# Experts taken in inner blocks of 1024 columns, with half of the small experts' gate units multiplied unsplit in plain fp32

## The reference

```python
def swiglu(xn, w_gate, w_up, w_down):
    return (jax.nn.silu(xn @ w_gate) * (xn @ w_up)) @ w_down

def moe_swiglu(xn, w_router, w_gate, w_up, w_down):
    logits = (xn @ w_router).astype(jnp.float32)
    top_v, top_i = lax.top_k(logits, TOP_K)
    top_w = jax.nn.softmax(top_v, axis=-1)
    gates = jnp.sum(jax.nn.one_hot(top_i, N_EXPERTS, dtype=jnp.float32) * top_w[..., None], axis=-2)
    out = jnp.zeros_like(xn)
    for e in range(N_EXPERTS):
        ye = swiglu(xn, w_gate[e], w_up[e], w_down[e])
        out = out + gates[..., e:e + 1].astype(xn.dtype) * ye
    return out
```

## Time and profile before

| | |
|---|---|
| time, median of 3 runs (range) | 1371.85 us (1371.69 to 1371.88) |
| the profiled execution's own time | 1372.46 us |
| its span, first to last instruction | 1370.7 us |
| busy: PE, PEld, DVE, ACT, POOL | 97%, 79%, 84%, 69%, 5% |
| mean granted TensorE clock | 0.997 of full speed |
| moved by DMA | 422.46 MB |
| chain that ended last: PE, DVE, ACT, issue | 75%, 16%, 4%, 3% |
| splits `split_lo` (DVE) of 2048 columns | 382, together 868.0 us |
| splits `split_hi` (ACT) of 2048 columns | 385, together 732.4 us |

### The profile page before, as it was taken

The page is one execution under the profiler, slowest core; times in us unless marked ns, Lnnn a source line. Parts: engine busy times, 40 slices in busy tenths (PEclk is TensorE's granted clock), DMA queues, the critical chain, the costliest instruction groups (busy, mean ns, idle before and its releaser), DMA issues.

```text
span 1370.7 us, 17261 instructions
## 1 busy us (share of the span) xinstructions
PE 1325.2 (97%) x6404; PEld 1083.2 (79%) x6404; DVE 1154.4 (84%) x970; ACT 951.4 (69%) x874; POOL 71.5 (5%) x110
## 2 busy tenths in 40 slices
PE   8999999999998999999999999999999999999998
PEld 7776888888886887777777767788888888888887
DVE  6897655557888989999999999998898899889886
ACT  5676544446775777777777777777777777776775
POOL 2120910000200000000000000000000000000000
PEclk9999999999999999999999999999999999999999
DMA  8743765555298989999999999999999999999980
GB/s 301 268 131 84 259 205 191 184 186 170 76 368 308 336 299 367 388 395 394 393 393 390 377 394 395 391 362 382 334 354 369 372 359 363 383 332 338 381 325 31
DMA packets 197860, 422.46 MB, mean 308 GB/s; under 512 B 13064, under 2 KB 37392, under 8 KB 197776
## 3 DMA queue, kind: packets, MB, share of 16 engines
q1 hardware_dynamic: 197776, 421.35, 85.1%
HBM read 420.27 MB, written 1.05 MB: 307 GB/s over the span
## 4 chain that ended last, share of the span: by engine, by line
PE 75%; DVE 16%; ACT 4%; issue 3%; SPq 1%; DMA 1%; POOL 0%; ACTq 0%; DVEq 0%; POOLq 0%
PE ps L334 20%; PE ps L336 19%; PE ps L335 19%; DVE w_lo L314 11%; PE ps L885 5%; ACT w_hi L297 3%; PE ps L883 3%; PE ps L1048 1%; PE ps L865 1%; PE ps L1023 1%; PE ps L1049 1%; PE ps L862 1%; PE ps L882 1%; DMA raw<-in_attn_w_qkv_dram 1%; DVE resid L2128 1%
## 5 line engine op out<-in xcount | busy, mean ns | idle before, releaser
L314 DVE TENSOR_TENSOR w_lo<-raw,w_hi 128x2048 fp32r<-128x2048 f32 x382 | 868.0, 2291 | 132.0 <-ACT w_hi L297 130.7
L297 ACT ACTIVATE w_hi<-raw 128x2048 fp32r<-128x2048 f32 x385 | 732.4, 1914 | 127.9 <-PE ps L336 105.5
L334 PE MATMUL ps<-w_hi,xe 128*128 128x512 f32 x448 | 179.2, 400 | 6.9 <-DVE w_lo L314 6.9
L336 PE MATMUL ps<-w_hi,xe 128*128 128x512 f32 x448 | 175.2, 391 | 0.0
L335 PE MATMUL ps<-w_lo,xe 128*128 128x512 f32 x448 | 175.2, 391 | 0.0
L334 PE MATMUL ps<-w_hi,h_t_hi 128*128 128x512 f32 x360 | 141.0, 392 | 0.3 <-DVE w_lo L314 0.3
L336 PE MATMUL ps<-w_hi,h_t_lo 128*128 128x512 f32 x360 | 140.3, 390 | 0.0
L335 PE MATMUL ps<-w_lo,h_t_hi 128*128 128x512 f32 x360 | 140.1, 389 | 0.0
L334 PE MATMUL ps<-w_hi,xb 128*128 128x512 f32 x280 | 111.5, 398 | 1.9 <-DVE w_lo L314 1.9
L885 PE MATMUL ps<-a_all,w_hi 128*128 128x512 f32 x308 | 109.8, 396 | 0.0
L336 PE MATMUL ps<-w_hi,xb 128*128 128x512 f32 x280 | 109.2, 390 | 0.0
(11 more groups left out here) (319 smaller groups left out, 1854.2 us busy)
## 6 DMA issues: line engine op xcount, KB each, us to landing
raw<-in_moe_w_gate_dram SPq DMA_DIRECT2D x112, 1024.0 KB, 7.8
raw<-in_moe_w_up_dram SPq DMA_DIRECT2D x111, 1024.0 KB, 7.9
raw<-in_moe_w_down_dram SPq DMA_DIRECT2D x111, 1024.0 KB, 7.5
raw<-in_attn_w_qkv_dram SPq DMA_DIRECT2D x11, 1024.0 KB, 12.3
raw<-in_ffn_w_gate_dram SPq DMA_DIRECT2D x11, 1024.0 KB, 5.3
raw<-in_ffn_w_up_dram SPq DMA_DIRECT2D x11, 1024.0 KB, 5.4
raw<-in_ffn_w_down_dram SPq DMA_DIRECT2D x11, 1024.0 KB, 4.9
raw<-in_ple_w_gate_dram SPq DMA_DIRECT2D x8, 1024.0 KB, 7.0
```

The source lines that it names most:

```text
L297: nc.scalar.activation(w_hi[:, u % SPLIT, :], raw_slot(u), ACT.Copy).then_inc(hi_ready, 1)
L314: nc.vector.tensor_tensor(w_lo[:, u % SPLIT, :], raw_slot(u), w_hi[:, u % SPLIT, :].bitcast(F32), ALU.subtract).then_inc(lo_ready, 1)
L334: nc.tensor.matmul(out, x[0], w[0], start=first, stop=False)
L336: return nc.tensor.matmul(out, x[1], w[0], start=False, stop=last)
```

## The change

**Blocks.** The hidden columns are taken in four blocks of 1024, 1024, 1024 and 512 columns. A gate or up unit of a wide block is 2 chunks of 1024 columns (4 KB runs in memory) in place of 4 of 512. A wide block has 4 gate, 4 up and up to 4 down units of the block before; the blocks of a turn have 10, 12, 12 and 8 units. silu, product and transposes' sources are 1024 wide, the two halves' hidden parts lie in `h_t` and `p_t`; silu stands behind the split of unit 6 of the block, the product behind that of unit 10.

**Whole units.** In turns 1 to 3 the last two gate units of each wide block and the last gate unit of the narrow one (`WHOLE`, 7 of 42 units, 21 in all) are not split. TensorE waits for their landing alone and multiplies the raw weights in plain fp32 by `x_whole`, an unsplit copy of the tokens that ScalarE makes when it gathers them; their slot of `raw` comes free when TensorE has used them.

**Scatter.** All four quarters of a result go through bank 5: quarter q waits until quarter q-1 has been added. TensorE issues them in the second block behind units 2, 3, 5 and 6, VectorE adds them behind the splits of units 5, 6, 8 and 9 (`SCATTER_AT`, `ADD_AT`).

**Turn 0.** The sort goes to the second block behind the split of unit 4, the placing of gates and slots behind that of unit 7, and the two row splits behind those of units 11 and 13. The gathers are four pieces in three banks, one ahead of each down unit of the last block; ScalarE, not VectorE, copies the transposed picks.

```diff
+BLOCKS = 4
+BLOCK_AT = (0, 10, 22, 34)
+HALVES = (2, 2, 2, 1)
...
+WHOLE_WIDE, WHOLE_NARROW = (2, 3), (1,)
+WHOLE = [U_TURN + PER_EXPERT * (t - 1) + BLOCK_AT[b] + i for t in FEW_AT for b in range(BLOCKS)
+         for i in (WHOLE_WIDE if HALVES[b] == 2 else WHOLE_NARROW)]
...
         def split_hi(u, k=0, by=None):
 
+            if whole(u, k):
+                return
             load_wait(nc.scalar, u, k)
...
                 before_it = ring(u) - RAW
-                split_wait(eng, before_it if before_it < U_WIDE else before_it + EXTRA, k)
+                before_it = before_it if before_it < U_WIDE else before_it + EXTRA
+                if whole(before_it, k):
+                    eng.wait_ge(unit_used, before_it + 1 + PER_EXPERT * k)
+                else:
+                    split_wait(eng, before_it, k)
             eng.dma_start(dst, view).then_inc(landed[ring(u) % RAW], 16)
...
-                                  for half in range(2)]
+                for b in range(BLOCKS):
+                    views = []
+                    for w in (ge, ue):
+                        n0, n = 1024 * b, 512 * HALVES[b]
+                        chunk = 4 // HALVES[b]
+                        views += [expert_rows(w, e, c0, chunk, n0, n) for c0 in range(0, KD, chunk)]
+                    if b or not first:
+                        before_it = (b - 1) % BLOCKS
+                        views += [expert_rows(de, e if b else e_before, 8 * before_it + 2 * j, 2, 0, D)
+                                  for j in range(2 * HALVES[before_it])]
                     units += [(u + n, view) for n, view in enumerate(views)]
...
 
                 pe.wait_ge(y_lo_ready, t + 1 + k)
                 pe.wait_ge(pick_t_copied, t + 1 + k)
-                if q < 2 and t % 2 == 0:
-                    pe.wait_ge(xe_lo_ready, 2 * (t + 3 + k))
-                elif q < 2:
-                    pe.wait_ge(added, 4 * (t + k))
-                else:
-                    pe.wait_ge(added, 4 * (t + k) + q - 1)
+                if q:
+                    pe.wait_ge(added, 4 * (t + k) + q)
                 tt, half = q // 2, q % 2
                 for y, stop in ((y_hi, False), (y_lo, True)):
-                    last = nc.tensor.matmul(ps[:, 5 + q % 2, :], pick_t[:, tt * P:(tt + 1) * P],
+                    last = nc.tensor.matmul(ps[:, 5, :], pick_t[:, tt * P:(tt + 1) * P],
                                             y[:, 512 * half:512 * half + 512], start=not stop, stop=stop)
...
+            def gate_or_up(t0, b, n, i, k=0, few=False):
+
+                x, width = xb if t0 == 2 else xe, 512 * HALVES[b]
+                chunks = 4 // HALVES[b]
+                u = block_unit(t0, b) + n * KD // chunks + i
+                unit(u, k)
+                if b == 0 and n == 0 and t0 < 2:
+                    pe.wait_ge(xe_lo_ready, 2 * (t0 + k) + (i + 1 if t0 else i // 2 + 1))
+                if i == 0:
+                    pe.wait_ge((silu_ready, hidden_ready)[n], JF + BLOCKS * t0 + b + BLOCKS * k)
+                for c in range(chunks):
+                    d = chunks * i + c
+                    for half in range(HALVES[b]):
+                        out, w = ps[:, 6 * n + half, :], weights(u, c, 512 * half, 512, width)
+                        first, stop = d == 0, d == KD - 1
+                        if few and whole(u, k):
+                            at = c * width + 512 * half
+                            last = nc.tensor.matmul(out, x_whole[:, t0 - 1, d, :], raw_slot(u)[:, at:at + 512], start=first, stop=stop)
+                        elif few and n == 1:
+                            last = product_few(out, x[:, 2 * d * P + FEW:2 * d * P + FEW + P], w, first, stop)
+                        else:
+                            last = product(out, (x[:, 2 * d * P:(2 * d + 1) * P], x[:, (2 * d + 1) * P:(2 * d + 2) * P]), w,
+                                           first, stop)
+                last.then_inc(unit_used, 1)
+
+            def transpose_picks(t0, k=0):
...
-                        transpose_hidden(g, k, few)
+                for b in range(BLOCKS):
+                    units = 2 * HALVES[b]
+                    before_it, t_before = (b - 1) % BLOCKS, t0 if b else t0 - 1
+                    few_then = few if b else few_before
+                    late = t0 == 0 and b == 1
+                    for n in range(2):
+                        for i in range(units):
+                            gate_or_up(t0, b, n, i, k, few)
+                            if (n, i) == ((0, 2) if late else (0, 0)) and (t0 or b):
+                                transpose_hidden(t_before, before_it, 0, k, few_then)
+                            if (n, i) == ((1, 1) if late else (1, 0)) and (t0 or b) and HALVES[before_it] == 2:
+                                transpose_hidden(t_before, before_it, 1, k, few_then)
+                            if b == 1 and t0 and (n, i) in SCATTER_AT:
+                                scatter(SCATTER_AT.index((n, i)), t0 - 1, k)
+                            if b == 2 and (n, i) == (0, 1):
+                                transpose_picks(t0, k)
+                    if b == 1 and t0:
+                        pe.wait_ge(y_lo_ready, t0 + k)
+                    if b or t0:
+                        u = block_unit(t0, b) + 2 * units
+                        for j in range(2 * HALVES[before_it]):
+                            if b == BLOCKS - 1 and t0 != 1:
+                                gather_piece(j, t0, k)
+                            down(u + j, before_it, j, half_at(t_before, before_it), k, few=few_then)
+                            if end and b == BLOCKS - 1 and j == 1:
+                                transpose_hidden(t0, b, 0, k)
+
+            SCATTER_AT = ((0, 2), (0, 3), (1, 1), (1, 2))
 
             pe.wait_ge(xs_ready, XS_AT[4] + 4)
             gather_first()
...
+            def silus(t0, b, k=0):
+                at = JF + BLOCKS * t0 + b
+                used(block_unit(t0, b) + 2 * HALVES[b] - 1, k)
+                act.wait_ge(hidden_ready, at + BLOCKS * k)
+                if HALVES[b] == 2:
+                    nc.scalar.activation(two(expert_silu), ps[:, 0:2, :], ACT.Silu).then_inc(silu_ready, 1)
+                else:
+                    nc.scalar.activation(expert_silu[:, 0:512], ps[:, 0, :], ACT.Silu).then_inc(silu_ready, 1)
+
...
+                for b in range(BLOCKS):
+                    u, units = block_unit(t0, b), 2 * HALVES[b]
+                    before_it, t_before = (b - 1) % BLOCKS, t0 if b else t0 - 1
+                    few_then = few if b else few_before
+                    late = t0 == 0 and b == 1
+                    wide, wide_before = HALVES[b] == 2, HALVES[before_it] == 2
+                    for n in range(0 if b or t0 else 1, 2 * units + (2 * HALVES[before_it] if b or t0 else 0)):
                         split_lo(u + n + AHEAD, k)
-                        if t0 == 0 and f == 1 and n == 1:
-                            hidden_lo(g - 1, k)
-                    hiddens(g, u + 3, k)
-                    if f == 1 and t0:
-                        add_result(0, t0 - 1, k)
-                        add_result(1, t0 - 1, k)
-                    if f == 2:
-                        if t0 == 0:
-                            for tt in range(TT):
-                                dve.wait_ge(rows_split_hi, tt + 1)
-                                cols = slice(tt * D, (tt + 1) * D)
-                                nc.vector.tensor_tensor(a_lo[:, cols], xs[:, tt, :], a_hi[:, cols].bitcast(F32),
-                                                        ALU.subtract).then_inc(rows_split_lo, 1)
+                        if n == 1 and b == 1 and t0:
+                            result_lo(t0 - 1, k)
+                        if n == (3 if late else 1) and (t0 or b):
+                            hidden_lo(t_before, before_it, 0, k, few_then)
+                        if n == ((7 if late else 6) if wide else 4) and (t0 or b) and wide_before:
+                            hidden_lo(t_before, before_it, 1, k, few_then)
+                        if n == ((8 if t0 or b else 7) if wide else 4):
+                            hiddens(t0, b, k)
+                        if b == 1 and t0 and n in ADD_AT:
+                            add_result(ADD_AT.index(n), t0 - 1, k)
+                        if late and n == 2:
                             sort_experts()
-                        dve.wait_ge(pick_transposed, t0 + 1 + k)
-                        nc.vector.tensor_copy(pick_t[:, :], ps[:, 7, 0:TT * P]).then_inc(pick_t_copied, 1)
-                    if f == 3 and t0 != 1:
-                        dve.wait_ge(pick_transposed, t0 + 1 + k)
-                        picks(t0 + 1, 0, k, few=few_next[0])
-                        picks(t0 + 2, 1, k, few=few_next[1])
-                    if f == FB - 1 and t0 != 1:
-                        pair_lo(0, t0, k)
-                    if f or t0:
-                        split_lo(u + 4 + AHEAD, k)
```

(26 more changed lines are left out.)

308 lines of the change are left out of this document (143 added, 165 removed).

## The result

| | us, median | lowest to highest | ratio to before | 95% interval of the ratio |
|---|---|---|---|---|
| before | 1371.88 | 1371.69 to 1373.66 | | |
| after | 1425.54 | 1423.66 to 1428.78 | 1.0391 | 1.0378 to 1.0403 |

The change makes the kernel 53.7 us slower. The prediction said 1413, in a range from 1384 to 1430: the time lies in the range, but over the forecast's own band (1404 to 1420) and in that of its rival 1 (1420 to 1432).

What follows compares the result with a forecast made beforehand. The prediction took full turns as bound by TensorE and small turns as hanging on VectorE's splits. From the median 1371.85, -4.7 (turn 0) + 27.5 (small turns) + 19.2 (scatters) = +42.0 gave 1413 us, range 1384 to 1430.

Steps and rivals of the forecast that it cites:

- the forecast's own band: Whole kernel: the time falls in 1404 to 1420 us, given a chance of 0.50.
- rival 1: Second blocks of turns: the clock falls at the new waits, 7 x 1.4 = +9.8 us, giving 1423; chance 0.12.
- Whole units: Small turns: 3.44 us a unit against 2.78 split, 21 add 13.9 us to TensorE; VectorE can't use all it is spared.
- The wide block: Wide small block of 12 units: 33.1 us against 31.1 for two earlier blocks, 2 us slower.
- Scatters: Second block: quarters 1 and 3 wait for adds, 2.35 and 2.45 us in full turns (+19.2 over four), 1.2 and 3.1 in small.
- Small turns together: Turns 1 to 3: longer by 9.2, 8.6 and 9.0 us, with 0.7 at the seam, +27.5 in sum.
- Turn 0: Turn 0: TensorE's stop and slow clock, 7.0 us, become 2.3 by the new order: -4.7, at worst 0, at best -7.
- The sum takes it as kept: TensorE's clock: assumed to stay at 1.00 through new waits of 2.4 to 3.1 us, so no cost was added.
- PEclk at 1.00 behind the waits: Full turns: TensorE's clock stays at 1.00 behind two waits for adds of 2.3 us each.
- the seam: Where turn 1 follows turn 0, whose down units are full: another 0.7 us.
- Rival 2: Only one loss is real: early enough adds give 1384 to 1395, or small turns add only +14, 1400; chance 0.20.
- Rival 3: Small turns: VectorE catches up during whole units with more than two split units in hand, adds hide, -15, 1357; chance 0.14.

Runs made afterwards that it cites:

- both: The changed kernel with the four adds one split earlier in VectorE's list and no whole units: 1370.20 us, 0.9979 of before.
- the clock held: The changed kernel with unread bf16 matmuls on a free bank ahead of the waits of scatter quarters 1 and 3: 1414.28 us, 1.0304 of before.

## Why the prediction was right, and where its sum was short

Step by step, by the prediction's own terms:

- **Whole units: right.** Two of them in a row take 6.9 us, 3.44 each, as worked out from the earlier trace rows. The first line shows their first six instructions:

```profile
573.67 2.74 PE L1123 MATMUL ps<-raw,xs 128*128 128x512 f32 x6
...
580.13 0.79 PE L1085 MATMUL ps<-w_hi,xe 128*128 128x512 f32 x1
```

  They start at 573.67, and the second matmul behind them starts at 580.77, one step of 0.23 after 580.54 (the record of the first, at 580.13, overlaps the last of them). Leaving out all 21 gave back 13.8 us, and putting 21 into before cost 14.9; the term said 13.9. That VectorE can't use what it is spared shows in its timeline, where each split beside whole units waits for ScalarE, and ScalarE, at 580.80, for the whole unit:

```profile
575.65 2.29 DVE L338 TENSOR_TENSOR w_lo<-raw,w_hi 128x2048 fp32r<-128x2048 f32 x1 [3.98 <-ACT w_hi L319]
579.30 2.29 DVE L338 TENSOR_TENSOR w_lo<-raw,w_hi 128x2048 fp32r<-128x2048 f32 x1 [1.36 <-ACT w_hi L319]
582.75 2.29 DVE L338 TENSOR_TENSOR w_lo<-raw,w_hi 128x2048 fp32r<-128x2048 f32 x1 [1.15 <-ACT w_hi L319]
```

```profile
580.80 1.92 ACT L319 ACTIVATE w_hi<-raw 128x2048 fp32r<-128x2048 f32 x1 [1.25 <-PE ps L1123]
582.62 1.00 ACT L1437 ACTIVATE tmp<-ps 128x1024 f32<-128x1024 f32 x1
583.52 3.79 ACT L319 ACTIVATE w_hi<-raw 128x2048 fp32r<-128x2048 f32 x2
```

- **The wide block: right in time, wrong in its name.** The walk through it gave 33.1; it took 33.35 (566.93 to 600.28), the narrow one 21.65 where 21.6 was said, and the silu does stand between the high parts of units 6 and 7. The prediction set its 2 us over before down to eight units of 8 matmuls in a row, as if width were the cause. Without whole units the same wide block of "both" takes 31.97 (559.50 to 591.47) against 31.1: 1.4 of the 2.2 are the two whole units and 0.8 the width. With their other blocks the wide blocks cost only 2.3 in all three small turns together, and seven whole units cost 4.9 to 5.1 a turn in narrow blocks.
- **Scatters: right.** 2.35 and 2.45 were said for full turns; the stops are 2.26 and 2.53 in turn 4, 1.98 and 2.38 in turn 5. For small turns 1.2 and 3.1: 1.24 and 3.20. With the clock held the full turns cost +19.8 (5.8, 4.4, 4.4, 5.2), said was +19.2.
- **Small turns together: right.** +27.5 was said. With the clock held they cost +27.2 (9.2, 8.2, 9.8).
- **Turn 0: right.** -4.7 was said, -5.0 measured.
- **The step that failed is "The sum takes it as kept".** The clock fell seven times, and that is the missing part: 1413 said, 1414.28 with the clock held, 1425.54 without. Its sign, PEclk at 1.00 behind the waits, failed with it. Rival 1 had the mechanism and, at 1423, the nearer time (7 x 1.4 = +9.8 against a measured 7 x 1.6 = 11.3), but got a chance of 0.12. That its count was right is luck: it took one fall in each second block, and there were none in turn 3, two in turn 5, and other counts in other executions. That the sum met the kernel with the clock held within 1.3 us is in part luck too: for turn 1 it had 120.4 (119.7 and the seam) from a base of 110.5, and the runs have 121.1 from a base of 111.9, so that two errors cancel. The argument against rival 1, that the waits end soon after, was none: before, the one long stop had shown that the clock falls, and nothing showed that 2.4 to 3.2 us were short enough. Waits up to 1.5 us were the only ones known to be harmless, so rival 1 should have had about the chance of the forecast, and the forecast been nearer 1418. The Trainium skill (page "TensorE: Matmul & The Clock Gate", section "HAM oscillation") said that waits between bursts put the clock back each time; the trace of after agrees, with PEclk down to 0.59 behind such waits, though not at each of them; the waits told of there are for DMAs and longer than most of these.

Rival 2 in its first half, adds that come early enough, was 1384 to 1395; with the tuple changed it is what the chip did, at 1384.0. Rival 3 is refuted by its own condition, more than two split units in hand: when the whole units ended at 580.5, VectorE had unit 4 ready and unit 5 in work (579.30 to 581.59), and with a third slot in use the gain was 4.8 us.

**Left open:** what decides whether the clock falls at a given wait. It fell after the one of 1.98 us at 1039.77, and not after the 2.26 us at 909.75, nor after the same 1.98 us in turns 6 and 7, nor in turn 3 of after behind 3.2 us. No run here tells them apart. Open too is whether whole units would pay with more than three slots.

## What to carry to other kernels

Where one engine works through a list in a fixed order, ask of every short step that another engine waits for which long step stands just ahead of it, and what that one itself waits for: an add of 0.74 us behind a split cost 41.5 us here, and moving a tuple of four numbers by one gave it back. To relieve the busiest engine helps only if the engines around it run ahead meanwhile; here, with a lead of two units, 46 us of spared VectorE time brought nothing, and the turns got longer by what TensorE paid. And a wait of about 2 us or more that is new on a busy TensorE should be priced with the fall of its clock on top.

## What the runs showed of the hardware

- The clock fell to its lower level (matmuls 0.43 apart in place of 0.23) after idle stretches of TensorE of 1.93 us (turn 3 of the kernel without whole units), 1.98 us (turn 5 of after) and more, though not after each of them; never, in the expert turns, after those of up to 1.6 us. A fall of after cost 1.6 us, by the kernel that kept TensorE busy with small bf16 matmuls in the waits, at PEclk 1.00 (1414.28 against 1425.54 us). One fall in the kernel without whole units lasted some 7 us, about twice as long.
- Falls differ between executions of the same program: after and the kernel without whole units, with seven falls each in their traces, spread over 5.1 and 3.9 us, the kernels without any over 0.6 to 1.5.
- In the small turns of after the loads of 4 KB runs came mostly at 405 to 422 GB/s in the stretches of 4 us in which they filled the DMA engines, gate, up and down units alike (410 in the stretch from 552 above), and those of the narrow block's gate and up units, in 2 KB runs, at 387:

```profile
836.00:840.00 4.00, 3.58 (x15) 2.63 (x15) 4.00 (x3) 3.64 (x2) 0.00 (x0) 1.00 1.05 387
```

  In the small turn of 113.3 us above, with before's blocks, the mean is 394.
